# Spatial gating with 1/rms applied behind its matmuls, and VectorE's weight split moved behind the next unit's row maxima

## What is computed

```python
def rms_norm(x, g):
    y = xf * lax.rsqrt(jnp.mean(xf * xf, axis=-1, keepdims=True) + EPS)
    return y.astype(x.dtype) * g

def spatial_gating_mixer(x, w_in, v_norm, w_s, b_s, w_out):
    z = jax.nn.gelu(x @ w_in)
    u, v = z[..., :SG_WIDTH], z[..., SG_WIDTH:]
    v = rms_norm(v, v_norm)
    v = v.reshape(bsz, s // SG_CHUNK, SG_CHUNK, SG_GROUPS, cg)
    w_masked = jnp.where(causal[None], w_s, jnp.zeros((), w_s.dtype))
    mixed = jnp.einsum("gts,bcsgk->bctgk", w_masked, v) + b_s.T[None, None, :, :, None]
    return (u * mixed.reshape(bsz, s, SG_WIDTH)) @ w_out

    # second block, per layer
    h = h + 0.5 * swiglu_2(rms_norm_2(h, norm_g[i, 0]), ffn1_wi[i], ffn1_wo[i])
    # three attentions ya, yb, yc on columns of rms_norm_2(h, ...) @ w_in[i]
    merged = (jax.nn.sigmoid(ga) * (ya @ w_branch[i, 0])
              + jax.nn.sigmoid(gb) * (yb @ w_branch[i, 1])
              + jax.nn.sigmoid(gc) * (yc @ w_branch[i, 2]))
    h = h + merged @ w_out[i]
```

## Time and profile before

| | us |
|---|---|
| runs | 3452.34, 3454.48, 3454.96 (median 3454.48) |
| profiled execution, its own time | 3455.64 |
| its span, first to last instruction | 3453.8 |
| TensorE busy | 3306.4 (96%) |
| VectorE, ScalarE, GpSimd busy | 1840.5, 1565.8, 169.5 |
| mean granted TensorE clock | 0.985 of full |

### The profile page before, as it was taken

The page is one execution under the profiler, slowest core; times in us unless marked ns, Lnnn a source line. Parts: engine busy times, 40 slices in busy tenths (PEclk is TensorE's granted clock), DMA queues, the critical chain, the costliest instruction groups (busy, mean ns, idle before and its releaser), DMA issues.

```text
span 3453.8 us, 39651 instructions
## 1 busy us (share of the span) xinstructions
PE 3306.4 (96%) x16391; PEld 2751.6 (80%) x16391; DVE 1840.5 (53%) x2378; ACT 1565.8 (45%) x1918; POOL 169.5 (5%) x285
## 2 busy tenths in 40 slices
PE   8999999939999999999999999999999899999998
PEld 6888888827888888878888888876788788877886
DVE  4456454565545455454565454644554645545545
ACT  4344444424444434344344344465543544565444
POOL 0000000003000000020000000022000000121000
PEclk9999999969999999999999999999999999999999
DMA  6545555522656545565456555643365555633553
GB/s 213 184 159 182 183 181 192 164 73 73 199 171 196 190 145 175 189 202 189 164 160 201 176 195 184 176 136 108 130 203 165 177 184 180 168 105 116 186 188 110
DMA packets 323903, 576.23 MB, mean 167 GB/s; under 512 B 45257, under 2 KB 130332, under 8 KB 323596
## 3 DMA queue, kind: packets, MB, share of 16 engines
q1 hardware_dynamic: 321196, 566.71, 50.6%
q0 software_dynamic: 2384, 6.64, 0.8%
q10 hardware_dynamic: 144, 0.35, 0.0%
HBM read 571.53 MB, written 1.09 MB: 166 GB/s over the span
## 4 chain that ended last, share of the span: by engine, by line
PE 87%; DVE 6%; ACT 4%; issue 1%; DMA 1%; DVEq 0%; SPq 0%; ACTq 0%
PE up L1650 19%; PE up L1652 19%; PE up L1651 19%; PE acc L1650 8%; PE acc L1652 8%; PE acc L1651 8%; ACT w_hi L563 3%; DVE w_lo L940 2%; PE up L1925 1%; PE acc L1820 1%; PE up L2120 1%; DVE xT_lo L1052 1%; PE acc L1747 0%; ACT xT_hi L628 0%; ACT units L707 0%
## 5 line engine op out<-in xcount | busy, mean ns | idle before, releaser
L940 DVE TENSOR_TENSOR w_lo<-raw,w_hi 128x2048 fp32r<-128x2048 f32 x543 | 1244.6, 2293 | 1343.3 <-ACT w_hi L563 1341.0
L563 ACT ACTIVATE w_hi<-raw 128x2048 fp32r<-128x2048 f32 x543 | 1040.7, 1918 | 1432.5 <-PE up L1652 1070.0
L1650 PE MATMUL up<-w_hi,xT_hi 128*128 128x512 f32 (+1 forms) x2500 | 987.3, 395 | 49.0 <-DVE xT_lo L1052 19.7
L1652 PE MATMUL up<-w_hi,xT_lo 128*128 128x512 f32 (+1 forms) x2500 | 976.9, 391 | 0.0
L1651 PE MATMUL up<-w_lo,xT_hi 128*128 128x512 f32 (+1 forms) x2500 | 976.9, 391 | 0.0
L1650 PEld LDWEIGHTS up<-w_hi,xT_hi 128*128 128x128 f32 x2500 | 472.4, 189 | 160.7 <-issue 41.7
L1652 PEld LDWEIGHTS up<-w_hi,xT_lo 128*128 128x128 f32 x2500 | 472.6, 189 | 98.2
L1651 PEld LDWEIGHTS up<-w_lo,xT_hi 128*128 128x128 f32 x2500 | 472.9, 189 | 94.0
L1650 PE MATMUL acc<-w_hi,ff_hi 128*128 128x512 f32 x1216 | 480.8, 395 | 3.5 <-DVE ff_lo L1071 3.5
L1652 PE MATMUL acc<-w_hi,ff_lo 128*128 128x512 f32 x1216 | 474.1, 390 | 0.0
L1651 PE MATMUL acc<-w_lo,ff_hi 128*128 128x512 f32 x1216 | 473.3, 389 | 0.0
(11 more groups left out here) (280 smaller groups left out, 2336.7 us busy)
## 6 DMA issues: line engine op xcount, KB each, us to landing
raw<-in_ffn_down SPq DMA_DIRECT2D x88, 1024.0 KB, 4.8
raw<-in_ffn_gate SPq DMA_DIRECT2D x80, 1024.0 KB, 5.1
raw<-in_ffn_up SPq DMA_DIRECT2D x80, 1024.0 KB, 5.1
raw<-in_ffn_wi SPq DMA_DIRECT2D x80, 1024.0 KB, 5.2
raw<-in_ffn_wo SPq DMA_DIRECT2D x44, 1024.0 KB, 4.9
raw<-in_w_in SPq DMA_DIRECT2D x38, 1024.0 KB, 5.1
raw<-in_conv_w_in SPq DMA_DIRECT2D x24, 1024.0 KB, 5.2
raw<-in_w_branch SPq DMA_DIRECT2D x12, 1024.0 KB, 5.1
```

Source lines behind the costliest of these rows:

```text
L563: nc.scalar.activation(w_hi[n % RING][:], raw[n % RING][:], ACT.Copy).then_inc(hi_ready, 1)
L940: nc.vector.tensor_tensor(w_lo[n % RING][:], raw[n % RING][:], w_hi[n % RING][:].bitcast(F32), ALU.subtract).then_inc(lo_ready, 1)
L1650: pe.matmul(ps, lh, rh, start=start, stop=False)
L1652: return pe.matmul(ps, ll, rh, start=False, stop=stop)
```

## The change

In spatial gating, x is turned raw and 1/rms comes in behind the matmuls: as ScalarE's scale in the Gelu of v, and for the gate, whose tokens lie along the free dimension, by a multiplication with `rb`, 1/rms broadcast to all partitions by one matmul (ones by `diag`). The tiles' order becomes gate 0, gate 1, mix 0, mix 1, gate 2, down 0, mix 2, gate 3, down 1, mix 3, and then down 2 and 3 in halves with the next stage's first transposes between them. Banks are fixed: gates in up 0 and 1, mixing in up 2 and 3. In the mixing stages VectorE's `refill` moves from the end of each dense piece to behind the next step's row maxima. The diff, cut to its core:

```diff
-XS = ("ffn", "mla", "mix", "ple")
+XS = ("ffn", "mla", "sg", "mix", "ple")
+        sg_gate = [carve(3584 + 512 * i, 512) for i in range(2)]
...
+                us, ds = [up_tile(w, CW * c) for c in range(4)], [down_tile(wo, CW * c) for c in range(4)]
+                return t + [us[0], us[1], us[2], ds[0], us[3], ds[1], ds[2], ds[3]]
...
         # ScalarE
+                act.wait_ge(rs_ready, seen.next(rs_ready))
                 for g in range(2):
                     consumed(n0 + 2 * g)
-                    consumed(n0 + 2 * g + 1)
+                    act.wait_ge(tile_used, seen.next(tile_used))
                     for t in range(NT):
+                        last = nc.scalar.activation(xn[:, t, 512 * g:512 * g + 512], up[2 * g + t][:],
+                                                    ACT.Gelu_apprx_tanh, scale=rstd[:, t:t + 1])
                     last.then_inc(v_ready, 1)
+                    split_hi(n0 + 2 * g + 1 + RING)
+                def gated(c):
+                    act.wait_ge(sg_scaled, seen.next(sg_scaled))
+                    nc.scalar.activation(sg_gate[c % 2], sg_gate[c % 2], ACT.Gelu_apprx_tanh).then_inc(gate_ready, 1)
...
         # VectorE, spatial gating
+                def scaled(c):
+                    if c >= 2:
+                        dve.wait_ge(prod_ready, prods + c - 1)
+                    nc.vector.tensor_tensor(sg_gate[c % 2].rearrange("p (m n) -> p m n", m=2),
+                                            up[c % 2][:].rearrange("p (m n) -> p m n", m=2),
+                                            rb[:].rearrange("p (o n) -> p o n", o=1).broadcast_to([P, 2, TOK]),
+                                            ALU.mult).then_inc(sg_scaled, 1)
...
         # VectorE, mixing stage
                     if part + 1 == KINDS[KIND[name]]:
                         evict(name)
-                    refill()
...
                             score_unit(i, (-HSCALE, -HSCALE), tab[:, 128:256], tab, negsinks[:, at:at + 1] if br == 2 else BIG)
+                    refill()
                     if 0 <= i - 1 < NU:
                         row_sums(i - 1, sink=UNITS[i - 1][0] == 2)
...
+                refill()
                 for piece in PIECES[STEPS][:-1]:
                     dense(*piece)
+                    refill()
                 merged_lo(0)
                 dense(*PIECES[STEPS][-1])
+                refill()
...
         # TensorE
+                drain_banks()
+                first_pair(n0, FW, [up[0][:], up[1][:]])
+                pe.wait_ge(diag_ready, seen.next(diag_ready))
+                pe.matmul(acc[2][:, 0:TOK], ones[:], diag[:].rearrange("p t n -> p (t n)"), start=True,
+                          stop=True).then_inc(rb_done, 1)
...
+                pair(n0 + 2, [up[2][:], up[3][:]])
+                gate_tile(n0 + 4, 0)
+                gate_tile(n0 + 5, 1)
+                mixing(0)
+                mixing(1)
+                gate_tile(n0 + 6, 2)
+                down(n0 + 7, 0, True, False)
+                mixing(2)
+                gate_tile(n0 + 8, 3)
+                down(n0 + 9, 1, False, False)
+                mixing(3)
+                halves = [(n0 + 10, hT_hi[:, 0], hT_lo[:, 0]), (n0 + 11, hT_hi[:, 1], hT_lo[:, 1])]
+                for j in range(2):
+                    pe.wait_ge(lo_ready, seen.next(lo_ready))
+                    pe.wait_ge(hlo_ready, seen.next(hlo_ready))
+                    down_half(*halves[j], 0, j == 1)
...
+                down_half(*halves[0], 1, False).then_inc(tile_used, 1)
+                residuals[0] += 1
+                turn_x(0)
+                down_half(*halves[1], 1, True)
```

More of the change, by code:

```diff
@@ L912, in _ @@
                 elif s[0] == "sg":
-                    sg(s, n0, bank)
-                    bank = (bank + 12) % 4
+                    sg(s, n0)
                 elif s[0] == "tables":
@@ L1319, in mla, with sg, squares_of @@
                 pending.append(1.0)
-            def sg(s, n0, bank0):
+            def sg(s, n0):
+                broadcast_rstd()
+                consumed(n0)
+                consumed(n0 + 1)
+                def squares_of(g):
+                    dve.wait_ge(v_ready, seen.next(v_ready))
+                    for t in range(NT):
+                        last = nc.vector.tensor_tensor_reduce(prod[:], xn[:, t, 512 * g:512 * g + 512],
+                                                              xn[:, t, 512 * g:512 * g + 512], 1.0, 0.0, ALU.mult,
+                                                              ALU.add, ssh[:, 2 * g + t:2 * g + t + 1])
+                        step(last)
+                squares_of(0)
+                dve.wait_ge(rb_done, seen.next(rb_done))
+                step(nc.vector.tensor_copy(rb[:], acc[2][:, 0:TOK]))
                 for h in range(2):
@@ L1329, in sg @@
                 last.then_inc(ws_ready, 1)
[L1330 to L1339, removed]
+                consumed(n0 + 2)
+                dve.wait_ge(tile_used, seen.next(tile_used))
+                squares_of(1)
                 step(nc.vector.tensor_tensor(ssh[:, 0:2], ssh[:, 0:2], ssh[:, 2:4], ALU.add))
@@ L1362, in sg @@
                     product_parts(c)
-                    if c:
-                        consumed(n + 1)
+                prods = seen.n.get(prod_ready.name, 0)
+                dve.wait_ge(tile_used, seen.next(tile_used))
+                scaled(0)
+                split_lo(n0 + 3 + RING)
+                split_lo(n0 + 4 + RING)
+                dve.wait_ge(tile_used, seen.next(tile_used))
+                scaled(1)
+                product(0)
+                split_lo(n0 + 5 + RING)
+                dve.wait_ge(tile_used, seen.next(tile_used))
+                scaled(2)
+                product(1)
+                split_lo(n0 + 6 + RING)
+                consumed(n0 + 7)
+                dve.wait_ge(tile_used, seen.next(tile_used))
+                scaled(3)
+                product(2)
+                split_lo(n0 + 8 + RING)
+                product(3)
+                consumed(n0 + 9)
+                late.append(n0 + 10)
                 owed.append(n0 + 11)
@@ L1883, in sg @@
             def sg(s, n0):
+                drain_banks()
[3 more added lines that the diff above has]
+                          stop=True).then_inc(rb_done, 1)
                 pe.wait_ge(ws_in, seen.next(ws_in, 32))
-                for _ in range(KD // 2):
-                    next_pair()
                 for g in range(8):
```

80 lines of the change are left out of this document (38 added, 42 removed).

## The result

The changed kernel takes 3424.47 us (median of 4 runs, 3422.67 to 3425.60), the kernel before beside it 3453.41 (4 runs, 3450.05 to 3454.96): ratio 0.9913, 95% interval 0.9901 to 0.9926. That is 29 us less, where 3425 was forecast and a range of 3417 to 3438. The profiled execution took 3425.6 us, its span is 3423.8, 30.0 less than before, and the mean granted clock 0.987 after 0.985.

A forecast was written before the change was run, and what follows sets the result against it. TensorE, busy 96% of the span, was taken as the bound. Spatial gating -16.9 and mixing stages -13.0 sum to -29.9 us: 3455.64 profiled becomes 3425.7, as a median 3424.5, stated as 3425, range 3417 to 3438.

The forecast's parts named there:

- Entry: Way into spatial gating: the 12.1 us of fillers, turn and idle go, 2.7 of new work comes, -9.4 us.
- End: Last down tiles of spatial gating: VectorE's cover is nearly gone, the idle of 1.45 becomes 1.1, -0.3 us.
- Exit: Behind spatial gating: wait of 2.05 becomes 1.89 as in the mixing tails, -0.2; the clock stretch after 1316 goes, -1.7 us.
- Wait for v: Before spatial gating's mixing matmuls: a second gate tile removes the 3.63 wait, -3.6 us, and the clock stretch behind it, -1.7.
- Mixing stages: Both mixing stages: splits behind the row maxima shorten waits by 4.8 and remove a 1.7 clock stretch each, -13.0 us in all.
- Splits that come later cost nothing: Mixing stages: later splits have some 6 us free, so cost 0; if wrong in the densest steps, +10 us in all.
- The clock stretch after 2337: Half-clock stretch behind the scores' waits in each mixing stage: gone once 1.8 us of idle becomes 1.0, -1.7 a stage.
- That the mixing stages give little: Rival: row sums, block work and GpSimd still stand behind the split; gain 2 per stage, stretches stay, 3433.5 us; chance 0.13.
- VectorE as the bound: Rival in spatial gating: VectorE's 8.9 of 11 us per step brings three waits and a stretch, 3431 us; chance 0.12.
- A clock at 1.2 GHz throughout spatial gating: Rival, slower than before: short waits between fixed banks hold TensorE at half clock, 3463 us; chance 0.03.
- That it does nothing: Rival in spatial gating: TensorE waits for 1/rms, so the old wait only moves, 3454.5 us; chance 0.04.
- The two middle rivals: The rivals that the mixing stages give little (3433.5 us, chance 0.13) and that VectorE bounds spatial gating (3431 us, chance 0.12).

The follow-up runs named there:

- late_split: Changed kernel with the split of the tile released last moved behind the first half of the transposed x at three stage exits; 3420.92 us, ratio 0.9901.
- mix_only: Kernel before with only the mixing stages changed, spatial gating as before; 3438.97 us, ratio 0.9958.
- no_fill: Kernel before without the fillers in the norm ahead of spatial gating; 3458.50 us, ratio 1.0009.
- one_gate: Changed kernel with one gate tile instead of two ahead of the first mixing matmuls in spatial gating; 3424.57 us, ratio 0.9911.
- v_late: Changed kernel with one gate tile ahead of the mixing matmuls and, for v's second half, the split again ahead of Gelu and squares; 3432.08 us, one execution.
- sg_only: Changed kernel with `refill` back at its old place, so only spatial gating is changed; 3436.13 us, ratio 0.9953.
- step18: Changed kernel with the split back ahead of the row maxima in step 18 of each mixing stage only; 3428.24 us, ratio 0.9920.
- early_old: Changed kernel with the split at its old place in steps 0 to 10 of the mixing stages, new place after; 3437.36 us, ratio 0.9941.
- both_more: Changed kernel with the last split moved later at three exits and the mixing stages' split behind row sums and block work in every step; 3426.86 us, ratio 0.9917.
- best: Changed kernel with late splits at three exits, `refill` behind the inverse row sums, and behind block work in step 1 alone; 3416.95 us, ratio 0.9882.
- after_again: The changed kernel, unedited, timed again on the same chip for comparison with a faster variant; 3423.21 us, ratio 0.9906.
- sums_first: Changed kernel with `refill` moved behind the inverse row sums in the mixing stages; 3421.87 us, ratio 0.9908.

## Why the prediction was right, and where it was not

The number: 3425 was said, 3424.5 measured. That they agree to 1 us is in part luck: the changed kernel's own four runs span 3 us, and errors below cancel. By its own steps:

- **Spatial gating, -16.9 said, -16.9 measured.** The sum is closer than its terms. *Entry*: no filler, no turn, idle 0.18; right. *End*: 1.45 was to become 1.1 and became 0.76, 0.3 better. *Exit*: 1.89 was said and 2.25 came, 0.4 worse. I had taken it from the mixing tails, since the form is the same. late_split removes 2.25 and 1.92 by one edit, so the wait is the same too; what makes it 0.3 longer here was not tried. The two errors nearly cancel. What is left of the 16.9, with 3.6 for v and 3.4 for the two clock stretches, is 9.4 for the entry, the term as it was said, and 9.5 by its own rows. One term was luck: the stretch behind the old exit's 2.05. The exit in mix_only and in no_fill is the old one, with 2.05 again, and neither has a stretch there. So that 1.7 belongs to the one execution that was read, and not surely to the change. The stretch behind 3.63 is another matter: all four executions with a wait of 3.6 or 3.7 for v have it.
- **Wait for v, -3.6 said and measured, with the wrong cause.** The step "before, one gate tile stood between the v tiles and the mixing matmuls; now there are two" gave the second tile as what removes it. one_gate and v_late give it 0.9, and 2.8 to the Gelu and squares that no longer stand behind a split. I had named that order on ScalarE in half a sentence, as an extra. The size came out because the change does both, and the sum took the whole wait as gone; that it gave this to the wrong one of the two did not show in the total.
- **Mixing stages, -13.0 said, -13.5 measured.** 1.48 to 0.94 (0.9 said), 0.81 and 1.75 to nothing (as said), 1.04 to 0.30 (0.2 said), the 1.8 at the scores to 0.82 (1.0 said), with GpSimd as the releaser that the step named. sg_only, step18 and early_old show the split's place as the cause of each.
- **Splits that come later cost nothing: right**, for this place. No idle in the mixing stages names `w_lo`, other than the 0.15 to 0.18 at their entry, which was there before. both_more shows what the bound was there for: moved once more, a split costs 1.02 at `w_lo`.
- **The clock stretch after 2337, -1.7 a stage: right in size for these two profiles, wrong in its reason.** The step said "nowhere in this trace is there one behind less" than 1.8 us of idle, and drew a threshold from that. One execution can't give one: sg_only has stretches behind 1.49, best behind 0.62, and step18 has none behind 1.21, 0.19 and 0.39. As an average the term holds for this place: in the old order such a stretch follows in six of six stages (before, sg_only, no_fill). The two stretches of spatial gating (1.7 each) are gone in this execution, but the exit's 2.25 could have brought one as it did before: one_gate has one behind 2.27.
- **The rivals.** That the mixing stages give little is refuted by sg_only against the changed kernel (14 us). VectorE as the bound: 0.76 is the only wait in the middle of spatial gating, so no. A clock at 1.2 GHz throughout spatial gating: the window shows 1.00. That it does nothing: 29 us. The two middle rivals were given 0.25 together; the order of VectorE's instructions, which the diff and the rows gave, would have borne less.

## What to carry to other kernels

Where an engine that executes in order feeds the bound one, put long work whose own reader is far off (here 2.29 us of splitting) behind what the bound engine waits for, place by place: it gave 6.7 us a stage and took 1.7 to 2.1 us of idle off each exit, and the move behind still more work (both_more) gave back what the exits had gained. When a wait has two possible causes, the size of the gain doesn't tell them apart; undo one alone. Price a clock stretch by how often it follows its kind of wait over several executions, not by the one profile at hand.

## What the runs showed of the hardware

**The same short idle has a clock stretch behind it in one execution and none in the next.** In these stages the granted clock falls to 0.50 for 3.4 us, or 6.8, behind an idle of TensorE. Over eight mixing stages with the old early waits (two each of before, sg_only, no_fill and early_old) the stretches sum to 3.4, 3.4, 10.2, 10.2, 10.2, 3.4, 0 and 3.4 us in this order, on average 5.5 a stage. Half of it, 2.8 us, is the most that it costs. Entry to exit it is less, because a wait behind a stretch can shrink: in the three stages with a stretch behind the 1.49, the next wait of 0.81 has no row. sg_only's first mixing stage takes 314.5 us (2161.54 to 2476.00) with 10.2 of stretches, the kernel before's 312.4 with 3.4, which is 310.7 without. So the 10.2 cost 3.8 and not 5.1, and over the eight stages the average is 2.3 us. Over sixteen stages of the eight profiles with all the new places or nearly (after, after_again, mix_only, sums_first, late_split, one_gate, v_late, best) there was one inside the stage, best's of 3.4 behind 0.62. The same 1.75 has a stretch in one stage of early_old and none in the other:

```profile
2988.60:2991.90 3.30, 3.30 (x11) 3.22 (x10) 0.52 (x4) 1.57 (x8) 0.98 (x2) 0.50 0.86 276
```

The length of the idle alone does not tell. Counted over all profiles, a stretch stands behind the scores' waits (1.21, 0.19, 0.40) in six of eight stages, behind 1.4 to 1.5 in three of eight, behind 1.75 in two of eight, and behind the exits' 1.9 to 2.3 in five of thirty-three.

So the removal of a short wait is worth more than the wait, by an amount that differs between executions. By these profiles it is some 2.2 us a stage beside 5.0 of idle (the 6.7 of the stages above less the 1.7 of their stretch). The Trainium skill's page on TensorE, "TensorE: Matmul & The Clock Gate", section "Part 1: The HAM clock gate", states that the point of transition differs from run to run; the runs agree in that the same kernel's stretches differ. Its section "HAM oscillation — how this bites in real kernels" warns of long idle gaps alone; here stretches stand behind 1.49, 1.75 and 1.89, so the measurement asks for more care than the page. What decides whether one comes is left open; no run here was made to show it.
